# First mixer of an HGRN2/GLA decoder step: the conditioning product in two batches of eight tiles per iteration instead of five batches of three and four

## The reference, cut to what matters

```python
cs = jax.nn.silu(c)
mod = (cs @ w_ada[l] + b_ada[l])[:, None, :]        # 2048 -> 6 * 2048, per layer
sh1, sc1, g1, sh2, sc2, g2 = jnp.split(mod, 6, axis=-1)
h = x * (1.0 + sc1) + sh1
q, f_pre, i, g = jnp.split(h @ w_in, 4, axis=-1)    # mixer of layer 0, 16 heads of 128
...                                                 # gated linear recurrence, per head
x = layer_norm(ALPHA * x + (1.0 + g1) * y, ln_w[l, 0], ln_b[l, 0])
```

## Time and profile before

| | |
|---|---|
| median of 3 runs | 3106.55 us (3106.01 to 3108.89) |
| the profiled execution: its own time, its span | 3104.89 us, 3103.1 us |
| PE busy | 3023.2 us, 97% |
| DVE busy, ACT busy, POOL busy | 1741.6, 1310.7, 301.0 us |
| loads of `w_ada` | 384 of 512 KB |
| loads of the first mixer's input weight | 128 of 512 KB |
| mean granted TensorE clock | 0.991 of full speed |

### The profile page before, as it was taken

The page is one execution under the profiler, slowest core; times in us unless marked ns, Lnnn a source line. Parts: engine busy times, 40 slices in busy tenths (PEclk is TensorE's granted clock), DMA queues, the critical chain, the costliest instruction groups (busy, mean ns, idle before and its releaser), DMA issues. The chain is left out here.

```text
span 3103.1 us, 65656 instructions
## 1 busy us (share of the span) xinstructions
PE 3023.2 (97%) x26684; PEld 2838.0 (91%) x26684; DVE 1741.6 (56%) x2487; ACT 1310.7 (42%) x1723; POOL 301.0 (10%) x290
## 2 busy tenths in 40 slices
PE   6899999999999999999999999999999999999998
PEld 3689999989899999999999899998999999999998
DVE  2477776665744444444446667666574454444445
ACT  1355555553533343333333544544354343343433
POOL 0022111110300000000001402210130000000000
PEclk8999999999999999999999999999999999999999
DMA  9998788888786686776885875675545555555552
GB/s 374 320 309 265 254 260 267 272 292 281 247 292 211 206 263 211 239 242 199 258 256 162 258 236 182 193 237 179 172 134 167 166 164 167 166 164 167 165 165 77
DMA packets 541631, 685.57 MB, mean 221 GB/s; under 512 B 22225, under 2 KB 469257, under 8 KB 541065
## 3 DMA queue, kind: packets, MB, share of 16 engines
q1 hardware_dynamic: 485602, 627.59, 62.8%
q10 hardware_dynamic: 55760, 54.04, 5.4%
HBM read 650.88 MB, written 30.67 MB: 220 GB/s over the span
## 5 line engine op out<-in xcount | busy, mean ns | idle before, releaser
L1958 DVE TENSOR_TENSOR w_lo<-raw,w_hi 128x1024 fp32r<-128x1024 f32 x804 | 992.7, 1238 | 1160.0 <-ACT w_hi L1328 1156.6
L1328 ACT ACTIVATE w_hi<-raw 128x1024 fp32r<-128x1024 f32 x804 | 849.6, 1059 | 1494.5 <-PE main L599 1189.0
L597 PE MATMUL main<-a_hi,w_hi 128*128 128x288 f32 x4224 | 1274.3, 302 | 11.9 <-DVE a_lo L2493 8.3
L599 PE MATMUL main<-a_hi,w_lo 128*128 128x288 f32 x4224 | 1247.4, 295 | 0.0
L598 PE MATMUL main<-a_lo,w_hi 128*128 128x288 f32 x4224 | 1246.4, 295 | 0.0
L597 PEld LDWEIGHTS main<-a_hi,w_hi 128*128 128x128 f32 x4224 | 795.5, 188 | 45.9 <-issue 28.8
L598 PEld LDWEIGHTS main<-a_lo,w_hi 128*128 128x128 f32 x4224 | 795.0, 188 | 4.6 <-issue 1.9
L599 PEld LDWEIGHTS main<-a_hi,w_lo 128*128 128x128 f32 x4224 | 794.8, 188 | 0.0
L597 PE MATMUL main<-act_hi,w_hi 128*128 128x288 f32 x2048 | 605.9, 296 | 0.0
L599 PE MATMUL main<-act_hi,w_lo 128*128 128x288 f32 x2048 | 604.9, 295 | 0.0
L598 PE MATMUL main<-act_lo,w_hi 128*128 128x288 f32 x2048 | 601.8, 294 | 0.0
(11 more groups left out here) (332 smaller groups left out, 2051.6 us busy)
## 6 DMA issues: line engine op xcount, KB each, us to landing
raw<-in_w_ada SPq DMA_DIRECT2D x384, 512.0 KB, 5.0
raw<-in_w_up SPq DMA_DIRECT2D x256, 512.0 KB, 4.0
raw<-in_w_down SPq DMA_DIRECT2D x256, 512.0 KB, 3.6
raw<-in_hg_w_in SPq DMA_DIRECT2D x128, 512.0 KB, 6.8
raw<-in_gla_w_in SPq DMA_DIRECT2D x100, 512.0 KB, 4.3
raw<-in_hg_w_out SPq DMA_DIRECT2D x32, 512.0 KB, 8.1
gl_s<-in_state_gla ACTq DMA_DIRECT2D x32, 512.0 KB, 5.7
out_new_gla_sample<-gl_s ACTq DMA_DIRECT2D x32, 512.0 KB, 4.7
```

The costliest lines, as they stand in the source:

```text
L597: mm(out, hi, x_hi[:, kb, :], start=kb == 0, stop=False)
L599: last = mm(out, lo, x_hi[:, kb, :], start=False, stop=kb == KB - 1)
L1328: F(w_hi[:, st.split_slot(g)].rearrange("p k n -> p (k n)"), raw[:, slot, :], ACT.Copy).then_inc(hi_ready, 1)
L1958: V.tensor_tensor(w_lo[:, s].rearrange("p k n -> p (k n)"), raw[:, slot, :], w_hi[:, s].rearrange("p k n -> p (k n)").bitcast(F32), ALU.su ...
```

## The change

The table of the first mixer becomes {4: 8, 13: 8}: eight "a" tiles in stop 4, eight in stop 13, ahead of levels 2 and 3. Each batch makes a sum of its own: the first in b5, the second in b7. ACT copies the first in step 8, the second in step 14. The transposes, now four, move from stop 12 to the end of stop 15. DVE adds the bias to the first sum and then the second sum to that (`mod_halves`, four additions with a wait for its own result between), behind the last level product of the iteration and no longer in step 13. Waits follow the buffers: the second batch waits until DVE has read the sample states out of b7, `hg_sample_state` and level 1 wait for the first copy alone. The order of the loads changes with the table: the weights of steps 7 to 14 now take the slots of the first batch, and the first seven weights of the next iteration, with its first "a" tile, those of the second.

```diff
-HG = Stage(None, HG_PAIRS, 16, {3: 3, 4: 3, 5: 3, 6: 3, 7: 4}, "AVAV", lead=4 * KB, opening=HG_OPENING)
+HG = Stage(None, HG_PAIRS, 16, {4: 8, 13: 8}, "AVAV", lead=4 * KB, opening=HG_OPENING)
...
             if L == 1 and prev:
-                pe.wait_ge(ada_copied, ADA_HG + n)
+                pe.wait_ge(H["ada_half"], n)
...
                     first = HG.first_ada(s)
-                    if first == 0 and prev:
+                    if first == 0:
                         pe.wait_ge(H["level_read"], 9 * n - 1)
-                    for i in range(first, first + HG.ada[s]):
-                        ada(HG, n, i, i, b5, 0, i == 0)
+                    else:
+                        pe.wait_ge(H["ss_read"], 4 * n)
+                    last = first + HG.ada[s] - 1
+                    for i in range(first, last + 1):
+                        ada(HG, n, i, i, b7 if first else b5, 0, i == first, last=last)
...
-                if s == 12:
-                    if prev:
-                        pe.wait_ge(H["ss_read"], 4 * n)
-                    ada_turn(ADA_HG + n, [b7[:, 0:P], b7[:, P:2 * P]], hg["ada"])
+                if s == 15:
+                    ada_turn(ADA_HG + n, [b7[:, i * P:(i + 1) * P] for i in range(4)], hg["ada"])
...
                 elif s == 8:
-                    hg_ada_copy(HG.ada_tile(n, KB), ADA_HG + n)
+                    act.wait_ge(ada_used, HG.ada_tile(n, 8))
+                    act.wait_ge(ada_turned, ADA_HG + n - 1)
+                    F(hg["ada"][:, 0:256], b5[:, 0:256], ACT.Copy).then_inc(H["ada_half"], 1)
...
+                if s == 14:
+                    act.wait_ge(ada_used, HG.ada_tile(n, KB))
+                    F(hg["ada"][:, 256:512], b7[:, 0:256], ACT.Copy).then_inc(ada_copied, 1)
...
+        def mod_halves(layer, block0, count, src):
...
+            for s_ in range(2):
+                last = V.tensor_tensor(out[:, s_], ps[s_], bias[:, s_].unsqueeze(2).to_broadcast([P, 4, NSEQ]), ALU.add)
+            step(last)
+            for s_ in range(2):
+                last = V.tensor_tensor(out[:, s_], ps[2 + s_], out[:, s_], ALU.add)
+            last.then_inc(mod_ready, 1)
...
-                if s == 13:
-                    mod_update(0, 8 * n + 2 * KB, 1, ADA_HG + n, [b7])
...
             level_mul(H, hg, n, 7)
+            mod_halves(0, 8 * n + 2 * KB, ADA_HG + n, b7)
             silu_lin(H, 2 * n + 2, hg["g"][:, :, :], panel(HG, 3))
```

More of the change, by code:

```diff
@@ L372, in mixer @@
             "s_stored": [S(f"{m}_s_stored{i}") for i in range(stores)]}
-    H = mixer("hg", 2, 2, "gate_lin gate_mix gate_soft k_ready")
+    H = mixer("hg", 2, 2, "gate_lin gate_mix gate_soft k_ready ada_half")
     G = mixer("gl", 4, 2, "oi_done oi_read squared sq_summed low_read gk_done gk_read gk2_loaded gk2_set")
@@ L602, in gemm, with ada @@
             last.then_inc(tile_done, 1)
-        def ada(st, n, i, kb, bank, col, first, kind="a"):
+        def ada(st, n, i, kb, bank, col, first, kind="a", last=KB - 1):
             slot, count = st.ring(n, kind, i)
@@ L609, in ada @@
                 last = mm(bank[32 * j:32 * j + 32, col:col + 256], c_t[:, kb, :], raw[:, slot, j * 256:(j + 1) * 256],
-                          start=first, stop=kb == KB - 1, skip_group_check=True, tile_position=(0, 32 * j))
+                          start=first, stop=kb == last, skip_group_check=True, tile_position=(0, 32 * j))
             last.then_inc(ada_used, 1)
@@ L865, in hg_last_state, with hg_sample_state @@
                ).then_inc(H["ss_done"], 1)
-        def hg_sample_state(pn, x, ada_count):
+        def hg_sample_state(pn, x):
             h, half_ = divmod(x, 2)
@@ L875, in hg_sample_state @@
             elif x == 2:
-                pe.wait_ge(ada_copied, ada_count)
+                pe.wait_ge(H["ada_half"], pn + 1)
             else:
@@ L908, in hg_step @@
                 if 8 <= s <= 11:
-                    hg_sample_state(pn, s - 8, ADA_HG + n)
+                    hg_sample_state(pn, s - 8)
             if own:
@@ L1982, in mod_update @@
             last.then_inc(mod_ready, 1)
+        def mod_halves(layer, block0, count, src):
+            dve.wait_ge(ada_turned, count)
+            out = mod[:, layer, cols(block0, 8), :].rearrange("p (j s) q -> p s j q", s=2)
+            bias = b_ada[:, layer, cols(block0, 8)].rearrange("p (j s) -> p s j", s=2)
+            ps = [src[:, i * P:(i + 1) * P].rearrange("p (j q) -> p j q", q=32)[:, :, 0:NSEQ] for i in range(4)]
+            for s_ in range(2):
[4 more added lines that the diff above has]
+            last.then_inc(mod_ready, 1)
         V.memset(c_t[:, :, :], 0.0).then_inc(c_set, 1)
@@ L2820, in build_program @@
     block.__exit__(None, None, None)
-STEPS = {"hg_act": 9, "hg_dve": 7, "gl_act": 7, "gl_dve": 5, "mlp0_dve": 8, "mlp1_dve": 8}
+STEPS = {"hg_act": 9, "hg_dve": 8, "gl_act": 7, "gl_dve": 5, "mlp0_dve": 8, "mlp1_dve": 8}
 BOOT_LOADS = 8
```

## The result

The changed kernel takes **3119.79 us** (median of 5 runs, 3119.46 to 3121.47) against 3106.55 before: ratio 1.0045, 95% interval 1.0033 to 1.0056. It is 13 us slower. The forecast was 3113.7 in a range of 3102 to 3125, slower with a chance of 0.57. The profiled execution spans 3118.0 us, 14.9 more than before.

A forecast was written before the change was run, and what follows sets the result against it. PE, busy in all of 72.00 us, was taken as the bound. An iteration: +1.34 (stop 5) + 0.25 (stop 13) - 0.56 (PE's work) = +1.03 us; seven, +7.2, on the earlier median give 3113.7 us, range 3102 to 3125.

The forecast's parts named there:

- The mechanism: Step 4: weight 7 takes a 0's slot, lands late and delays the sample split that PE's stop 5 waits for.
- Landing: Step 4: weight 7 lands 4.0 us after SP issues its load, taken between 3.8 and 4.9.
- The wait in stop 5: Line 826: PE waits 1.34 us for DVE's sample split in each of seven iterations, between 0.9 and 2.2.
- level 5: Next iteration's weight 0, late in step 13, delays ACT and level 5: 0.25 us an iteration, from 0 to 0.9.
- last tile, a 15: Stop 13: it takes weight 15's slot, split in step 12, but PE needs it late enough; costed at nothing.
- a wait of line 609 in stop 13: Sign that the forecast is wrong: PE waiting for a DMA there, which the sum leaves at nothing.
- PE's own work: Batches save 0.84 us and transposes take 0.28 back: PE's work falls 0.56 us an iteration, 0.35 to 0.75.
- The fixed cost of 0.24: Stops 3, 5, 6 and 7: each batch between operations of another shape costs 0.24 us beside its tiles.
- The transposes: Moved from stop 12, four in their own stop cost 0.50 us against 0.22 for two: 0.28 us more an iteration.
- The first (weight 7 in time): Rival: no wait in stop 5, only PE's saving of 3.9 us is left, 3102.6 us; chance 0.15.
- The second (a further wait in the chain of levels): Rival: the chain into level 1 or level 5 short by 1 to 2 us each time, 3120 to 3128; chance 0.18.
- The third (the clock): Rival: the clock falls at each new wait, at least 7 x 0.8 us, 3119 or more; chance 0.07.

The follow-up runs named there:

- run 1: Changed kernel with ACT's and DVE's mixer work moved ahead of the cast and split of weight 7 in step 4: 3110.18 us, ratio 1.0016.
- run 4: Kernel before with only its batch table changed, to {4: 8, 6: 4, 7: 4}: 3114.28 us, ratio 1.0023.
- run 5: Kernel before with only its batch table changed, to {4: 7, 6: 4, 7: 5}: 3102.91 us, ratio 0.9992.
- run 7: Kernel before with table {4: 8, 6: 4, 7: 4} and mixer work ahead of cast and split in step 4: 3102.37 us (0.9988), then 3103.46 us (0.9991).
- run 3: Changed kernel with ACT's and DVE's mixer work moved ahead of the cast and split in steps 4 and 13: 3104.03 us, ratio 0.9995.
- run 6: Changed kernel with five batches, {3: 3, 4: 3, 5: 2, 6: 4, 7: 4}, both sums in b5, both copies in step 8: 3107.16 us, ratio 1.0004.
- run 10: Kernel before with table {4: 8, 7: 8} and mixer work ahead of the cast and split in step 4 alone: 3109.64 us, ratio 1.0015.
- run 9: Kernel before with table {4: 8, 7: 8} and mixer work ahead of the cast and split in steps 4 and 7: 3110.47 us, ratio 1.0012.

## Why the prediction was right, and where its sizes were off

**The mechanism** was the one forecast, and runs 1, 4, 5 and 7 show it from both sides. The size was not: 13.2 us where 7.2 stood, and the sizes that were off pull in both directions. The terms of stop 5, against the trace after:

- *SP's issue behind the first tile*: 0.89 us forecast from the earlier trace rows, 0.88 measured. *Landing*: 4.0 taken between the 3.8 and 4.9 of the earlier trace rows; the profile gives 4.0, 4.0 and 4.4 us for the loads of weight 7 in iterations 3, 4 and 5. The Trainium skill's estimate of 3.2 us (DMA: Bandwidth & Descriptors, Anatomy of one DMA), which the page gives for loads that GpSimd issues, is 0.8 short for this load of SP's, and with it the sum would have been 3108, no change.
- *Cast to sample split*: 3.20 us from the earlier trace rows, and 335.69 - 332.49 = 3.20 again.
- *The wait in stop 5*: 1.34 us forecast; 0.83 in the first iteration, 1.26 to 1.64 in the others, 9.0 us in seven where 9.4 stood. But a wait costs more than its idle time. The profile counts it from the modelled end of the matmul before, 0.16 us later than the next one would have started, and the first pair of line 826 then takes 0.51 us (335.79 to 336.30) in place of 0.43. So stop 5 is 10.7 us longer in all.

**Where the 6 us more come from.** The step that failed in size is the one on stop 13. It had two parts. For *level 5* I took 0.25 us an iteration from a span of 0 to 0.9; its idle time is 0.46 on the mean, and stop 15 is longer by 0.74 with what each wait costs beside it (5.2 us in seven, 0.5 of it one wait for `hg_near`, DVE's line 2150). The timelines of steps 13 to 15, iteration 3, answer to the earlier trace rows:

```profile
373.26 1.06 ACT L1329 ACTIVATE w_hi<-raw 128x1024 fp32r<-128x1024 f32 x1 [7.91 <-DMA raw<-in_hg_w_in]
374.22 0.40 ACT L1442 ACTIVATE hg_x<-hg_suf 128x256 f32<-128x256 f32 x1
...
380.24 0.46 PE L736 MATMUL bank<-hg_x 128*32 128x32 f32 x32 [0.37 <-DVE hg_x L2121]
```

The exponentials of level 4 start 6.63 us after the batch (367.59), where 5.95 was forecast: weight 0 takes 4.6 us to land where 4.0 was taken, with the last tiles of the batch still on their way.

For this *last tile, a 15*, I wrote "I cost it at nothing", and named a wait of line 609 in stop 13 as a sign that the forecast is wrong. The sign came. The tile takes the slot of weight 15, whose split DVE ends only at 365.44; the load needs 5.9 us from its issue, and PE wants the tile at 370.60. Iteration 1, where it was in time, and iteration 3:

```profile
220.96 3.66 PE L609 MATMUL bank<-raw,c_t 128*32 128x256 f32 x64
224.44 0.26 PE L631 MATMUL bank<-hg_x 128*32 128x32 f32 x6
...
371.56 0.64 PE L609 MATMUL bank<-raw,c_t 128*32 128x256 f32 x8 [0.68 <-DMA raw<-in_w_ada]
372.02 0.26 PE L631 MATMUL bank<-hg_x 128*32 128x32 f32 x6
```

In time, batch and levels are 3.48 us apart (220.96 to 224.44), late 4.43 (367.59 to 372.02). Five late ones make 2.1 us of idle time and 3.2 us in all. No run takes this lateness away by itself; its cost is read from the traces.

**The term that was off the other way** is PE's own work. I had it fall by 0.56 us an iteration; it falls by 1.0. An iteration of run 3 without any wait takes 70.68 us (line 767 at 388.62 and 459.30), one before 71.71. The batch of stop 4 is as forecast: 331.04 - 326.58 = 4.46 us with line 810, 3.45 more than without one, just 8 x 0.43. That of stop 13 has a fixed cost of 0.04 us and not 0.12. The fixed cost of 0.24 that I gave to all four of the others is 0.34 in stop 3 (2.42 us with its batch, 606.72 to 609.14, against 0.79 now, 321.98 to 322.77) and 0.31 in stop 6, and the weight product behind each starts 0.02 to 0.03 us slower. The transposes cost some 0.17 us net (0.15 in run 6) where I had 0.28.

The clock, last, fell once in the stage: from line 826 to the next line 841 PE needs 5.89 us there (483.32 to 489.21) and 4.37 an iteration earlier, so 1.5 us.

Against the forecast this is +1.3 (stop 5) + 3.4 (level 5) + 3.2 (last tile) + 1.5 (clock) - 3.3 (PE's work) = +6.1 us. The stage by the same terms grew by 10.7 + 5.2 + 3.2 + 1.5 - 7.2 = 13.4 us; the two traces differ by 13.6. Of the rest of the profiled execution, what follows the stage was 2.0 us longer and what precedes it 0.7 shorter, without any part in the change. That the total stayed within the range owes something to luck: without PE's larger saving it would have come 3 us nearer to its upper end.

**The rivals.** The first (weight 7 in time) did not come; the saving it counts on is there, but not clear of 0.2%: with both moves of run 3 the changed kernel is 2 us under the kernel before. The second (a further wait in the chain of levels) came at level 5 and not at stop 11, and small: it explains 3.4 us of the error. The third (the clock) came in part.

## What to carry to other kernels

In this ring of eight slots a batch of eight tiles makes the next load start only when the batch does. For a change of this kind find, for every load, whose slot it takes, and count from that use to the landing and on through all that stands behind its consumer in each in-order queue; do the same for the batch's own last tiles. A late load cost nothing where its first consumer stood last in its step (run 1, run 7), and where work for the next stop stood behind it, it cost what exceeded that work's margin (11 us in run 4, little in run 10). Moving two calls in two steps recovered what the change had lost. Making batches larger saved only the change of shape around them, 0.24 to 0.34 us each.

## What the runs showed of the hardware

**Short waits and the clock.** After the wait of 1.64 us at 483 us the granted clock fell, and 2 us windows of the changed kernel read (columns as in the earlier trace rows):

```profile
484.00:486.00 2.00, 2.00 (x13) 2.00 (x13) 2.00 (x3) 1.26 (x4) 0.00 (x0) 0.61 1.10 348
486.00:488.00 2.00, 2.00 (x10) 2.00 (x10) 0.74 (x1) 1.94 (x3) 0.00 (x0) 0.53 1.11 349
```

PE is busy throughout, at the lower level of 1.2 GHz for most of these two; the next window is at 1.00 again. The six other waits of line 826 in that trace, up to 1.46 us, left it at 1.00, and so did one of 1.74 us in run 9 (line 609, at 492). In run 4 the same stop waited 2.29 us once and the clock then stood at 0.50 for three windows (482 to 488), 3.1 us lost by the same count (7.45 us from line 826 to line 841 in place of 4.37). In the second trace of the changed kernel it did not fall behind stop 5 at all, but at 676 and 720 us, in the last steps of the mixer and the output projection. So a wait can cost in what follows about as much as in itself, or more; the length of the wait alone doesn't tell which one will, and these runs don't settle what does.

**A batch's fixed cost depends on its neighbours.** Between operations of another shape it is 0.24 to 0.34 us (stops 3, 5, 6 and 7). Behind the read-out of the same 128x32 stationary tiles (stop 4) it is zero, and ahead of levels of such tiles (stop 13) 0.04.
